# One phase for the first half of a diffusion block: norms, keys, queries, attention and convolution norm fused

## The reference, cut to what matters

```python
hx = modulate(rmsnorm(x, g_norm1), sh, sc);  hc = the same of ctx
k_c, v_c = mla_kv(hc @ w_in[:, :160]);  k_x, v_x = mla_kv(hx @ w_in[:, :160])
cq, zf, zc, zg = split(hx @ w_in[:, 160:])        # 256, 256, 512, 3072 columns
q_x = rope(rmsnorm(rmsnorm(cq, g_cq) @ w_uq, g_qn))      # 8 heads of 96
#     k = rope(rmsnorm([rmsnorm(ckv, g_ckv) @ w_ukv, kr], g_kn)), v the other half
a_x = softmax(q_x . [k_c, k_x] * 96 ** -0.5) @ [v_c, v_x]
x = x + gt * (g0 * (a_x @ wb_attn) + g1 * (fourier_mix(zf) @ wb_fnet)
              + g2 * (conformer_conv(zc) @ wb_conv)) @ w_out
# conformer_conv: u = a * sigmoid(g); 31 taps per channel; layernorm over 256 channels; silu
```

## Time and profile before

| what | value |
|---|---|
| median of 3 runs | 4361.96 us (4360.77 to 4363.42) |
| the profiled execution | 4361.22 us, span of its instructions 4359.4 us |
| granted TensorE clock, mean of the span | 0.897 of 2.4 GHz |
| PE, PEld, DVE, ACT, POOL busy | 82%, 61%, 57%, 15%, 27% of the span |
| HBM read | 1078.36 MB, 251 GB/s over the span |

### The profile page before, as it was taken

The page is one execution under the profiler, slowest core; times in us unless marked ns, Lnnn a source line. Parts: engine busy times, 40 slices in busy tenths (PEclk is TensorE's granted clock), DMA queues, the critical chain, the costliest instruction groups (busy, mean ns, idle before and its releaser), DMA issues. The chain is left out here.

```text
span 4359.4 us, 42922 instructions
## 1 busy us (share of the span) xinstructions
PE 3560.4 (82%) x14770; PEld 2645.5 (61%) x14770; DVE 2474.9 (57%) x4715; ACT 643.0 (15%) x1745; POOL 1192.8 (27%) x1036
## 2 busy tenths in 40 slices
PE   6889897689998999976896565332998899998899
PEld 3458685577777777765684222111776676776576
DVE  2555476887788667765547898887342301342301
ACT  2241111440000000012302111100101300001300
POOL 0000000135565566640004777776000000000000
PEclk8879998799999999997898777666999899999899
DMA  5318364589999999971467999998882244692243
GB/s 178 125 34 243 123 163 171 186 316 409 409 409 372 409 409 409 407 284 53 122 187 273 377 400 367 407 403 326 294 298 103 93 164 161 209 308 99 93 164 107
DMA packets 562471, 1096.83 MB, mean 252 GB/s; under 512 B 29748, under 2 KB 343092, under 8 KB 560982
## 3 DMA queue, kind: packets, MB, share of 16 engines
q1 hardware_dynamic: 410680, 554.12, 37.5%
q0 software_dynamic: 147456, 536.94, 31.6%
q10 hardware_dynamic: 4128, 3.15, 0.2%
HBM read 1078.36 MB, written 15.73 MB: 251 GB/s over the span
## 5 line engine op out<-in xcount | busy, mean ns | idle before, releaser
L1670 POOL DMA_INDIRECT gu<-in_u_tab,eid x256 | 347.4, 1357 | 980.1 <-DVE gate L1336 646.8
L2015 PE MATMUL ps<-gv,diag 128*128 128x512 f32 x512 | 302.1, 756 | 382.8 <-DMA gv<-in_v_tab,eid 240.1
L2514 PE MATMUL ps<-hT,wring 128*128 128x256 f32 x2560 | 561.4, 380 | 3.6 <-DMA wring<-in_ffn_w_up 3.5
L1634 PE MATMUL ps<-hT,wring 128*128 128x256 f32 x2048 | 488.6, 393 | 81.6 <-DVE hT L1820 80.3
L2514 PEld LDWEIGHTS ps<-hT,wring 128*128 128x128 f32 x2560 | 487.0, 190 | 87.8 <-issue 13.6
L1634 PEld LDWEIGHTS ps<-hT,wring 128*128 128x128 f32 x2048 | 391.6, 195 | 173.4 <-DVE hT L1820 119.6
L1625 PE MATMUL ps<-hT,wring 128*128 128x256 f32 x2048 | 462.8, 379 | 1.1 <-ACT G L1711 1.1
L2015 PEld LDWEIGHTS ps<-gv,diag 128*128 128x128 f32 x512 | 122.8, 247 | 560.2 <-issue 404.9
L1625 PEld LDWEIGHTS ps<-hT,wring 128*128 128x128 f32 x2048 | 389.0, 190 | 53.9 <-issue 1.1
L1844 DVE SCALAR_TENSOR_TENSOR wring<-gv,wgt,wring 128x1024 f32<-128x1024 f32 x254 | 326.3, 1285 | 110.5 <-DMA gv<-in_v_tab,eid 104.7
L1827 DVE CUSTOM_DVE_ANT_0 gu<-gu,htok 128x1024 f32<-128x1024 f32 x256 | 313.1, 1223 | 121.8 <-DMA gu<-in_u_tab,eid 119.5
(11 more groups left out here) (370 smaller groups left out, 4453.1 us busy)
## 6 DMA issues: line engine op xcount, KB each, us to landing
wring<-in_u_first SPq DMA_DIRECT2D x128, 512.0 KB, 9.2
wring<-in_v_tab SPq DMA_DIRECT2D x128, 512.0 KB, 6.8
room<-in_ada_w SPq DMA_DIRECT2D x32, 1536.0 KB, 11.7
wring<-in_ffn_w_gate SPq DMA_DIRECT2D x44, 1024.0 KB, 9.3
wring<-in_ffn_w_up SPq DMA_DIRECT2D x44, 1024.0 KB, 12.4
wring<-in_ffn_w_down SPq DMA_DIRECT2D x44, 1024.0 KB, 5.0
wring<-in_w_in SPq DMA_DIRECT2D x72, 512.0 KB, 6.7
wring<-in_w_mod SPq DMA_DIRECT2D x19, 1024.0 KB, 6.9
```

Source lines behind the costliest of these rows:

```text
L1634: m = nc.tensor.matmul(ps[:, n // 2, (n % 2) * S:(n % 2 + 1) * S], vslot[:, e % 2, n * P:(n + 1) * P], act_[:, e % 3, :], start=e == 0 and ...
L1670: nc.gpsimd.indirect_dma_start(gu[:, n % RING, :], None, ub, bass.IndirectOffsetOnAxis(ap=eid[:, n // COLS, n % COLS:n % COLS + 1], axis=0 ...
L2015: m = nc.tensor.matmul(ps[:, mixed_banks(t) + b, :], diag[:, s, i, :], gv[:, d + i, b * 512:(b + 1) * 512], start=first, stop=last)
L2514: m = mm(ps[:, b + n, q * S:(q + 1) * S], up_slot(s, q)[:, k, n * P:(n + 1) * P], hT[:, k, 0:S], start=k == 0, stop=k == KD - 1)
```

## The change

The phases from `norm_both` to `convolution_norm`, and `open_layer`, are replaced by one phase, `mixer`, without a barrier inside; the semaphores order the engines. Within it:

- The query latent's columns join the key latent's: 416 columns of `w_in` (160 for the context tiles of layer 1) are computed token-major, one product per feature block and token tile. So the latents' norms are sums along the free axis, taken by ACT while it squares (`latent_squares`, `accum_out`), and the sum of squares of the separate products with ones falls away. The normed latents are turned by transposes.
- `project` computes the other six units in the order 4, 2, 5, 3, 0, 1, laid between the other work of TensorE.
- The root of the block's norm is taken by ACT straight from the sum. ACT also squares keys and queries for their head norms. The gain of the 64 unrotated features goes onto the copy of the turned queries (the product of both gains, `gcols`), that of the 32 rotated ones into the tables `ropes`. Queries are not divided by their root: it multiplies the scores, inside the exponential (`rq`).
- The gate product of the convolution moves from POOL to DVE, and its 62 taps are spread: 18 after the first gate product, 6 before the attention, the rest over its steps. The convolution's norm lies in the last steps of the attention.
- Attention: DVE normalises the probabilities before they are turned; the values are then the stationary side, and the result comes out feature-major on 64 partitions per head, two heads to a bank. A context tile (half as many keys) takes two heads per step: 24 steps in layer 0, 16 in layer 1. TensorE turns step i-2 and applies the values of step i-3 after the scores of step i.
- Layer 0's sixteen modulation units move into the steps 1 to 17 of the attention, with three slots instead of six. The gains, the other weights and the tables are issued by SP at the start, behind one another on one queue; `wkvq` is 1.7 MB.

```diff
+    def mixer(self, l, T, mods=None):
...
+        for qt in range(min(tiles, 2)):
+            for h in range(H1):
+                steps.append((qt, h, 1, 0))
+        for qt in range(2, tiles):
+            for h in range(0, H1, 2):
+                steps.append((qt, h, 2, 2))
...
+        SOON, NEXT = 18, 24
+        LAST = n - 6
+
+        def tap_count(i):
+            return NEXT + (2 * TAPS - NEXT) * min(i, LAST) // LAST
...
+            @block.sync
+                sp.dma_start(wkvq, a["w_in"][l, :, 0:WK].rearrange("(k p) n -> p k n", p=P)).then_inc(wkd.sem, 16)
+                for i, name in enumerate(("g_qn", "g_kn")):
+                    sp.dma_start(gqk[:, i, :], a[name][l:l + 1, :].to_broadcast([P, QK])).then_inc(gaind.sem, 16)
+                sp.dma_start(gcols[0:QK, :], a["g_qk_cols"][l]).then_inc(gaind.sem, 16)
+                sp.dma_start(wp, a["w_in"][l, :, WK:ZG0].rearrange("(k p) n -> p k n", p=P)).then_inc(wpd.sem, 16)
+                sp.dma_start(wukv, a["w_ukv"][l]).then_inc(wud.sem, 16)
+                sp.dma_start(wuq, a["w_uq"][l].rearrange("(k p) n -> p k n", p=P)).then_inc(wqd.sem, 16)
+                sp.dma_start(dftf[:], a["dft_feature"]).then_inc(tabd.sem, 16)
+                sp.dma_start(dftt[:], a["dft_token"]).then_inc(tabd.sem, 16)
+                sp.wait_ge(pfull.sem, 6)
+                for i, hu in enumerate(half_units):
+                    if i >= 3:
+                        sp.wait_ge(rowed.sem, i - 2)
+                    sp.dma_start(mslot[i % 3], mods(hu, 256, 256)).then_inc(m_in[i % 3].sem, 16)
...
+            @block.tensor
...
+                def scores(i):
+                    qt, h, nh, kt = steps[i]
+                    w = 512 // nh
+                    if i >= 2:
+                        pe.wait_ge(eready.sem, i - 1)
+                    for c in range(nh):
+                        m = mm(ps[:, i % 2, c * w:(c + 1) * w], qT[0:QK, h + c, qt * P:(qt + 1) * P], kT[0:QK, h + c, kt * P:4 * P],
+                               start=True, stop=True)
+                    m.then_inc(sfull.sem, 1)
+
+                def turn(i):
+                    pe.wait_ge(pn.sem, i + 1)
+                    if i >= 2:
+                        pe.wait_ge(tcopied.sem, i - 1)
+                    for b in range(4):
+                        m = nc.tensor.transpose(ps[:, 6 + i % 2, b * P:(b + 1) * P], pr[i % 3][:, b * P:(b + 1) * P], ident[:])
+                    m.then_inc(tfull.sem, 1)
+
+                def values(i):
+                    qt, h, nh, kt = steps[i]
+                    nb = 4 // nh
+                    p = pair_of[i]
+                    pe.wait_ge(tcopied.sem, i + 1)
+                    if p >= 2:
+                        pe.wait_ge(od.sem, p - 1)
+                    for c in range(nh):
+                        at = 64 * ((h + c) % 2)
+                        for b in range(nb):
+                            m = mm(ps[at:at + 64, 4 + p % 2, 0:P], vtok[:, kt + b, h + c, :], pt[i % 2][:, (c * nb + b) * P:(c * nb + b + 1) * P],
+                                   start=b == 0, stop=b == nb - 1)
+                    m.then_inc(ofull.sem, 1)
...
+                latent(0)
+                latent(1)
+                pe.wait_ge(wpd.sem, 16)
+                project(0)
+                project(1)
+                turn_latents()
+                project(2)
+                project(3)
+                pe.wait_ge(wud.sem, 16)
+                up_keys(0, 8)
+                project(4)
+                project(5)
+                up_queries()
+                fourier()
...
+                heads(ktok, 4, 0)
+                pe.wait_ge(qn.sem, tiles)
+                heads(qtok, tiles, H1)
+                pe.wait_ge(branchd.sem, 2 * segs)
+                pe.wait_ge(headd.sem, 2 * H1)
+                for i in range(n + 3):
+                    if i < n:
+                        scores(i)
+                    if 2 <= i < n + 2:
+                        turn(i - 2)
+                    if i >= 3:
+                        values(i - 3)
+                    if 1 <= i <= NU:
+                        rows_of(i - 1)
+                    if 2 <= i <= NU + 1:
+                        columns_of(i - 2)
...
+            @block.scalar
...
+                root_of(0)
+                modulate(0, 0, 4)
+                root_of(1)
+                modulate(0, 4, KD)
+                modulate(1, 0, KD)
+                latent_squares(0)
+                latent_squares(1)
+                gate(0)
+                for i in range(3):
+                    latent_columns(i)
+                gate(1)
...
+                    if i == n:
+                        act.wait_ge(vsum.sem, 1)
+                        run(cvar, ps[:, 3, 0:T], ACT.Sqrt, bias=eps[:], scale=1.0 / CC).then_inc(croot.sem, 1)
...
+            @block.vector
...
+                dve.wait_ge(gaind.sem, 48)
...
+                glu(0)
+                some_taps(0, SOON)
+                glu(1)
...
+                def maximum(i):
+                    qt, h, nh, kt = steps[i]
+                    x = mneg[:, col_of[i]:col_of[i] + nh]
+                    dve.wait_ge(sfull.sem, i + 1)
+                    own(v.tensor_reduce(x, ps[:, i % 2, :].rearrange("p (c n) -> p c n", c=nh), AX, ALU.max))
+                    done(dve, v.tensor_tensor(x, x, rq[:, 1, 8 * qt + h:8 * qt + h + nh], ALU.mult), mready)
+
+                def normalize(i):
+                    nh = steps[i][2]
+                    w = 512 // nh
+                    r = rs[:, col_of[i]:col_of[i] + nh]
+                    dve.wait_ge(eready.sem, i + 1)
+                    own(v.reciprocal(r, r))
+                    for c in range(nh):
+                        x = pr[i % 3][:, c * w:(c + 1) * w]
+                        ins = v.tensor_scalar(x, x, r[:, c:c + 1], None, ALU.mult)
+                    done(dve, ins, pn)
...
+                for i in range(n + 1):
+                    if i < n:
+                        maximum(i)
                     if i:
+                        normalize(i - 1)
+                    if i < LAST:
+                        some_taps(tap_count(i), tap_count(i + 1))
...
-        self.norm_both(A_G1, 0, 1, self.key_weights(l))
...
-        self.keys_values(l, self.first_unit(w_in(KV_IN, 512)))
-        qtok = self.qtok
-        self.project(l, T, w_in(KV_IN, 512), self.half_units_ahead(mods) if l == 0 else None)
-        self.queries(l, T, mods if l == 0 else None)
...
-        self.attend(steps, QK ** -0.5, conv=T // S)
-        self.turn(lambda t, j: ao[:, t * 512 + j * P:t * 512 + (j + 1) * P], T // P, self.branch, 4)
...
-        self.convolution_norm(T // S, l == 0, ahead=lambda sp, landed: load(sp, 0, 0, landed))
+        self.mixer(l, T, mods if l == 0 else None)
```

More of the change, by code:

```diff
@@ L520, in _ @@
[L520 to L529 removed]
+                        pe.wait_ge(hready.sem, KD * c + k + 1)
@@ new lines, in up_keys @@
+                def up_keys(first, last):
+                    for i in range(first, last):
+                        t, j = divmod(i, 2)
+                        if i < 4:
+                            pe.wait_ge(latd.sem, max(i, 1))
+                        else:
+                            pe.wait_ge(kvd.sem, i - 3)
+                        mm(ps[:, 2 + (i + 3) % 4, :], ckvT[:, t * P:(t + 1) * P], wukv[:, j * 512:(j + 1) * 512], start=True,
+                           stop=True).then_inc(kvfull.sem, 1)
@@ L883, in turn @@
-    def turn(self, tok, tiles, dst, ntile, gain=None):
-        nc, ps, ident = self.nc, self.ps, self.ident
-        with self.phase("full", "copied") as (block, full, copied):
-            @block.tensor
-            def _(pe):
-                for j in range(ntile):
-                    if j >= 8:
-                        pe.wait_ge(copied.sem, j - 7)
-                    for t in range(tiles):
-                        m = nc.tensor.transpose(ps[:, j % 8, t * P:(t + 1) * P], tok(t, j), ident[:])
-                    m.then_inc(full.sem, 1)
-            @block.scalar
-            def _(act):
-                for j in range(ntile):
-                    act.wait_ge(full.sem, j + 1)
-                    nc.scalar.activation(dst[:, j, 0:tiles * P], ps[:, j % 8, 0:tiles * P], ACT.Copy,
-                                         scale=1.0 if gain is None else gain[:, j:j + 1]).then_inc(copied.sem, 1)
@@ new lines, in _ @@
+                for t in range(tiles):
+                    dve.wait_ge(qsq.sem, t + 1)
+                    done(dve, v.tensor_reduce(small[:, 32 + 8 * t:40 + 8 * t], sqh[t % 2], AX, ALU.add), qss)
+                    done(dve, rope(qtok, t, 0) if t < 2 else gain(qtok, t, 0), qn)
+                some_taps(SOON, NEXT)
+                r = small[:, 32:32 + 8 * tiles]
+                dve.wait_ge(qroot.sem, 1)
+                own(v.reciprocal(r, r))
+                done(dve, v.tensor_scalar(rq[:, 0, 0:8 * tiles], r, QK ** -0.5, None, ALU.mult), rqd)
```

904 lines of the change are left out of this document (397 added, 507 removed).

## The result

The changed kernel takes 4233.28 us (median of 4 runs, 4230.28 to 4238.94), the one before on the same chip 4362.35 (4360.77 to 4363.42): a ratio of 0.9706, 95% interval 0.9689 to 0.9723. Predicted were 4232. The span of the profiled execution went from 4359.4 to 4233.4, by 126.0.

A forecast was written before the change was run, and what follows sets the result against it. No engine is full: work passes between engines while PE waits, then runs at 1.2 GHz. Gains of 85.4 (layer 0) and 51.6 (layer 1), 137 less 7 for hand-offs, leave 130: median 4232 us, range 4208 to 4266.

The forecast's parts named there:

- Norm and start: Layer 0's norm: gains queued behind wkvq land at 44.5 us, reciprocal at 46, first scaled block for PE at 49.
- Latents: Layer 0's latent products: 22.4 us of PE plus 2 for a start at half clock, ending at 73.4.
- Middle: Layer 0's projections, keys, queries and Fourier mix: 70.6 us of PE without a pause, 1 added for ACT, ending at 145.0.
- Head transposes: Layer 0, before the attention: 16 heads, ACT-bound at 0.5 us each, and a hand-off of 0.6, ending at 153.6.
- Attention, layer 0: PE sets the step, 3.85 us with a modulation unit; 80.1 us in sum, last scores at 233.7.
- Tail: Layer 0, last scores to merge: 12.5 us, merge at 246.2 instead of 331.6, 85.4 gained.
- Layer 1: Second mixer, attention steps set by DVE at 3.62 us: merge at 2085.9 instead of 2137.5, 51.6 gained.
- The allowance: Both mixers: 7 us off the gain for hand-offs counted as free, 40 steps at 0.1 and some ten waits; 130 remain.
- The first: Attention: DVE waits for the exponential; steps 3.85 to 4.3 in layer 0, 3.62 to 4.5 in layer 1; 4248 us; chance 0.12.
- The second: Head transposes drop the clock, 7 us in layer 0, 3 in layer 1, attention starts slow: +11, 4243 us; chance 0.06.
- The third: Attention runs at half clock: layer 0 gains 60 us, layer 1's steps 24; 4316 us; chance 0.07.
- The fourth: Attention steps run one after the other, 8.7 us instead of 3.85 in layer 0: +165, 4397 us; chance 0.03.

The follow-up runs named there:

- e1: The changed kernel with the three transfers of the gains issued ahead of wkvq instead of behind it: 4270.11 us, ratio 0.9674 to the kernel before.
- e4: The changed kernel with all six projection units first, then latents' turns, keys and queries one after the other: 4294.51 us, ratio 0.9742 to the kernel before.
- e0: The changed kernel run again, unaltered, on another chip: 4230.41 us, ratio 0.9704 to the kernel before on that chip.
- e2: The changed kernel with the 38 of 62 convolution taps in the attention's steps left out: 4268.08 us, ratio 0.9677 to the kernel before.
- e6: The changed kernel with 40 taps instead of 24 ahead of the first scores: 4228.05 us, ratio 0.9699 to the kernel before.
- e3: The changed kernel with layer 0's sixteen modulation units in one stretch ahead of the head transposes: 4329.95 us, ratio 0.9808 to the kernel before.
- e7: The changed kernel with 40 taps ahead of the first scores and the gains issued ahead of wkvq: 4217.89 us, ratio 0.9673 to the kernel before.
- e8: The changed kernel with gains first, 40 early taps, the convolution norm's root by logarithm and exponential, SiLUs earlier: 4217.86 us, ratio 0.9679 to the kernel before.

## Why the prediction was right, point by point

The path was right in both layers, stage by stage. That the time came within 1.3 us of the forecast is in part luck: the two mixers gave 132.6 us where 137 were summed up and 130 forecast, the stretches that are not changed took 6.6 of it back in the first trace (spans 126.0 apart), and the medians came out 129.1 apart. Two traces of one kernel differ by 6.8 us between the mixers alone.

- **Norm and start.** The gains landed at 44.89 (44.5 predicted), reciprocal at 46.62 (46), latents at 49.88 (49). e1 shows that the gains cause it. Before, the reciprocal stood at 44.16: the removed step was lost to the queue, as said.
- **Latents.** 24.6 us with 0.91 of clock; 24.4 predicted.
- **Middle.** 70.2 us without a pause of PE; predicted 70.6 and 1 for ACT. The 1 us for ACT was not paid. The cover named there (key norms beside units five and six) was tested by e4: without it some 15 us in both layers, where the prediction named about 30 us of DVE.
- **Head transposes.** 9.4 instead of 8.6. The copies to `qT` take 4.74 for eight instead of 4.00, with a scale on them.
- **Attention, layer 0.** 84.4 instead of 80.1: the term of the sum that was mis-sized. The step is 3.96 instead of 3.85: scores 0.94 (0.86), turn 0.53 (0.49), values 1.02 (0.94), modulation 1.47 (1.54). Scores cost 0.08 more than two records inside one group, turn and values 0.04 and 0.08 more than in the kernel before, where the groups follow one another in another order; why was not tried. Thirteen steps make 1.4 us of it. The filling with the first such step took 11.7 us (11.25 predicted), the one step with columns alone 3.0 (3.4). The last steps cost 2.8 more (18.2 instead of 15.4): PE waits there for VectorE and ScalarE, which have the convolution's norm in their order. The price varies: in the second trace of the same kernel (e0) the clock fell in those steps (0.75 from 238 to 242), the last sum took 3.30 us instead of 1.98, and the attention 85.7.

```profile
234.59 0.66 PE L578 MATMUL ps<-ident,wring 128*128 128x128 f32 x4 [1.10 <-DVE wring L945]
235.71 0.66 PE L591 MATMUL ps<-wring,vtok 128*64 128x128 f32 x8 [0.47 <-ACT branch L767]
236.66 1.98 PE L655 MATMUL ps<-ktok,ones 128*128 128x512 f32 x4 [0.28 <-ACT ktok L832]
```

- **Tail.** 13.0 instead of 12.5; reciprocal 3.35, as in the earlier trace rows. The merge's first weights stayed hidden.
- **Layer 1.** 141.9 instead of 142.6. The step is 3.72 instead of 3.62, by DVE as predicted (e2, e6). The head transposes took 7.6, as predicted (7.5). Two terms missed and cancelled: the attention took 49.4 us instead of 51.3, the tail 11.5 instead of 9.6.
- **The allowance** of 7 us for hand-offs: layer 0 fell 5.2 short of its 85.4, in the heads, the attention and the tail, and layer 1 gained 0.8 more than its 51.6. So 4.4 were used, and by mis-sized steps more than by the hand-offs that the 7 were meant for.
- **Rivals.** The first (DVE waits inside the steps) did not occur in layer 0, where PE has no idle; DVE stands in layer 1 only for its own work. The second (clock in the head transposes) did not happen in the changed kernel: the window 144.70:154.10 is at 1.00 with nothing but transposes, and so is the start of layer 0's attention in both traces. It is not refuted in general. In e1, e3, e4, e7 and e8 layer 0's attention starts at about 0.5 for 7 us or more, right behind the transposes and a wait of 1.7 us for ACT, and in e1, e4 and e7 that costs 1.4 us (first to fifth scores 13.1 instead of 11.7); in layer 1 the changed kernel itself has 0.58 from 1954 to 1960. In e1 the instructions from the latents to the scores are the same, only their times differ. So full clock at that place was luck, of a size well inside the range. The rule weighed in the prediction, that full clock doesn't engage for transposes, fails in e3: they start at 0.50 and, with nothing else on PE, rise to 1.00. The third (attention at half clock) is refuted by 1.00 over 66 us, and yet its ground was sound: e3 shows the same units at half clock when they run alone. The fourth (steps one after the other) is refuted by 3.96. The transposes of e3, in two windows:

```profile
193.00:197.00 4.00, 4.00 (x21) 3.82 (x20) 0.00 (x0) 2.37 (x4) 0.00 (x0) 0.50 1.16 299
198.00:202.00 4.00, 4.00 (x37) 3.68 (x36) 0.00 (x0) 4.00 (x8) 0.00 (x0) 1.00 0.21 52
```

## What to carry to other kernels

Sum each stage by the engine that is full in it: the same 38 taps were free in one layer and cost 10.5 us in the other. An interleaving that leaves TensorE's work unchanged was worth some 15 us here through the engines that it gives time to finish, so list what each wait in an order covers before undoing it. Small transfers that gate a chain belong ahead of a large load on the same queue: three loads of 48 KB and less, behind one of 1.7 MB, cost 10.6 us of stage time in two uses.

## What was not expected of the hardware

- Products that put four narrow tiles beside one another ran at 1.2 GHz over some 37 us when alone (1.94 us per sixteen), once two waits had let the clock fall, while the same products between attention steps ran at 2.4 GHz (1.07). It cost no time that the runs show, as the transfers came at 3.0 us per unit.
- Transposes alone held full clock for 9.4 us with PE at 7.65 of them, and rose from 0.50 to 1.00 in e3. Behind them, in layer 0, the clock fell to 0.50 for about 7 us in five experiments and stayed at 1.00 in the changed kernel (two traces), e2 and e6, after the same wait of PE. What decides it was not tried.
- One of the three chips of the experiments needed 52 to 57 us more for the kernel before (4415 against 4363 and 4358). In the traces taken on it the mixers have their usual lengths and the stretch behind the second one is 42 to 55 us longer (2266.4 to 2279.8 against 2224.5). Why was not tried.
